# Experts' weights issued from two engines: ScalarE for the even units, SyncE for the odd units and each expert's first

## What is computed

```python
def moe_ffn(h, p, j):
    logits = (h @ p['w_router'][j] + p['b_router'][j]).astype(jnp.float32)
    top_v, top_i = lax.top_k(logits, TOP_K)                 # TOP_K = 2 of N_EXPERTS = 8
    gates = jax.nn.softmax(top_v, axis=-1)
    combine = jnp.einsum('blk,blke->ble', gates, one_hot(top_i))
    out = jnp.zeros_like(h)
    for e in range(N_EXPERTS):
        act = jax.nn.silu(h @ p['we_gate'][j, e]) * (h @ p['we_up'][j, e])   # 1024 x 1408 each
        out = out + combine[..., e:e + 1] * (act @ p['we_down'][j, e])       # 1408 x 1024
    return out
```

## Time and profile before

| | before |
|---|---|
| median of the runs (lowest, highest) | 924.25 us (922.62, 925.26) |
| profiled execution, its time | 925.9 us |
| profiled execution, its span | 924.2 us |
| mean granted TensorE clock | 0.977 |
| TensorE matmul busy | 874.5 us (95%) |
| VectorE busy | 711.6 us (77%) |
| ScalarE busy | 561.3 us (61%) |
| moved by DMA | 240.74 MB, mean 260 GB/s |
| first matmul of the experts to their last | 508.8 to 904.1 us |
| experts' units | 144: 104 of 1 MiB, 32 of 768 KB, 8 of 512 KB |

### The profile page before, as it was taken

The page is one execution under the profiler, slowest core; times in us unless marked ns, Lnnn a source line. Parts: engine busy times, 40 slices in busy tenths (PEclk is TensorE's granted clock), DMA queues, the critical chain, the costliest instruction groups (busy, mean ns, idle before and its releaser), DMA issues.

```text
span 924.2 us, 14135 instructions
## 1 busy us (share of the span) xinstructions
PE 874.5 (95%) x5414; PEld 778.2 (84%) x5414; DVE 711.6 (77%) x928; ACT 561.3 (61%) x633; POOL 47.0 (5%) x98
## 2 busy tenths in 40 slices
PE   4999999999999999999996999999999999999993
PEld 4997989999999999977885787888887888888881
DVE  4898895755546437978876889888888988888988
ACT  5427985444434335059952867686867777777751
POOL 2000012100000001010102000000000000000040
PEclk9999999999999999899997999999999999999998
DMA  8821137996345556510354789999999999999981
GB/s 332 338 92 44 42 129 290 395 418 249 135 176 212 185 177 251 224 48 1 112 221 162 271 316 391 376 357 385 371 382 341 390 368 389 371 385 355 378 312 49
DMA packets 39864, 240.74 MB, mean 260 GB/s; under 512 B 5016, under 2 KB 5368, under 8 KB 19056
## 3 DMA queue, kind: packets, MB, share of 16 engines
q1 hardware_dynamic: 32432, 208.01, 59.7%
q0 software_dynamic: 5936, 27.19, 7.6%
q10 hardware_dynamic: 1440, 4.77, 1.3%
HBM read 215.01 MB, written 25.51 MB: 260 GB/s over the span
## 4 chain that ended last, share of the span: by engine, by line
PE 80%; ACT 9%; DVE 7%; issue 2%; DMA 1%; DVEq 0%; ACTq 0%
PE ps L499 10%; PE ps L500 10%; PE ps L501 10%; PE ps L797 9%; PE ps L798 9%; PE ps L799 9%; PE ps L811 4%; PE ps L813 4%; PE ps L812 4%; PE ps L515 2%; ACT whi L926 1%; PE ps L872 1%; PE ps L449 1%; DVE low L336 1%; PE ps L819 1%
## 5 line engine op out<-in xcount | busy, mean ns | idle before, releaser
L1641 DVE TENSOR_TENSOR low<-raw,whi 128x2048 fp32r<-128x2048 f32 (+1 forms) x144 | 300.1, 2110 | 47.6 <-ACT whi L1160 47.2
L1160 ACT ACTIVATE whi<-raw 128x2048 fp32r<-128x2048 f32 (+1 forms) x144 | 252.9, 1781 | 74.7 <-DMA raw<-in_w_experts 54.9
L499 PE MATMUL ps<-nhi,whi 128*128 128x264 f32 x560 | 161.8, 289 | 16.8 <-DVE low L336 13.0
L926 ACT ACTIVATE whi<-raw 128x2048 fp32r<-128x2048 f32 (+1 forms) x60 | 109.2, 1826 | 109.9 <-PE ps L501 108.7
L336 DVE TENSOR_TENSOR low<-raw,whi 128x2048 fp32r<-128x2048 f32 (+1 forms) x60 | 130.5, 2180 | 45.5 <-ACT whi L926 45.4
L500 PE MATMUL ps<-nlo,whi 128*128 128x264 f32 x560 | 160.3, 286 | 0.0
L501 PE MATMUL ps<-nhi,low 128*128 128x264 f32 x560 | 159.6, 285 | 0.0
L797 PE MATMUL ps<-whi,ehi 128*128 128x512 f32 (+1 forms) x384 | 147.1, 383 | 0.2
L798 PE MATMUL ps<-low,ehi 128*128 128x512 f32 (+1 forms) x384 | 145.0, 378 | 0.0
L799 PE MATMUL ps<-whi,elo 128*128 128x512 f32 (+1 forms) x384 | 144.8, 377 | 0.0
L499 PEld LDWEIGHTS ps<-nhi,whi 128*128 128x128 f32 x560 | 106.5, 190 | 18.2 <-issue 16.8
(11 more groups left out here) (389 smaller groups left out, 1352.1 us busy)
## 6 DMA issues: line engine op xcount, KB each, us to landing
raw<-in_w_experts SPq DMA_DIRECT2D x104, 1024.0 KB, 6.9
raw<-in_w_dense SPq DMA_DIRECT2D x54, 1024.0 KB, 5.1
raw<-in_w_experts SPq DMA_DIRECT2D x32, 768.0 KB, 6.3
xs<-zero POOLq DMA_DIRECT2D x5, 2560.0 KB, 32.0
Cs<-in_state_c POOLq DMA_DIRECT2D x2, 2064.0 KB, 11.2
out_new_s<-Cs POOLq DMA_DIRECT2D x2, 2064.0 KB, 8.2
raw<-in_w_experts SPq DMA_DIRECT2D x8, 512.0 KB, 6.8
xe<-xs SPq DMA_DIRECT2D x7, 512.0 KB, 8.8
```

Of the source, the lines that this page charges most:

```text
L499: pe.matmul(o, hi[:, k, c], h_k, start=first, stop=False)
L926: act.activation(whi[:, u % NHI, 0:n], raw[:, u % NRAW, 0:n], ACT.Copy).then_inc(hi_done, 1)
L1160: act.activation(high_slot(odd, c)[:, 0:kt * w], raw[:, c % NRAW, 0:kt * w], ACT.Copy).then_inc(hi_done, 1)
L1641: dve.tensor_tensor(low[:, c % NRAW, part], raw[:, c % NRAW, part], high_slot(odd, c)[:, part].bitcast(F32), ALU.subtract).then_inc(lo_don ...
```

## The change

In the experts, the units with even numbers are issued by ScalarE. Each expert's unit 0 stays with SyncE, and so do units 0 to 5 of the first expert. ScalarE issues unit `c + 2` in `expert_hi` of unit `c`: first it waits for TensorE's unit `c - 4`, which is what frees both the high part's slot for unit `c` and the slot of `raw` for unit `c + 2`; then it issues the DMA; then it waits for unit `c`'s landing and converts it. For this the wait for `used` moves ahead of the wait for the landing, for all units. SyncE skips those units, and keeps the load of `xe` at its place.

```diff
+        def by_act(it, c):
+
+            return c % 2 == 0 and c > (NRAW - 1 if isinstance(it, int) and it == 0 else 0)
+
...
                         sp.dma_start(xe[:, :], block_of(xs, it + 1)).then_inc(S["xe_in"], 16)
+                    if by_act(it, c):
+                        continue
                     sp.wait_ge(used, it * NU + ND + c - NRAW + 1)
...
-            def expert_hi(it, c, odd=False):
+            def expert_hi(it, c, odd=False, e=None):
                 _, g, k0, kt, w = EU[c]
+                act.wait_ge(used, it * NU + ND + c - (3 if isinstance(it, int) and it == 0 and c < 3 else 4) + 1)
+                if e is not None and c + 2 < NU and by_act(it, c + 2):
+                    n = EU[c + 2][3] * EU[c + 2][4]
+                    src = a["w_experts"][bass.ds(e, 1), c + 2, :, 0:n].rearrange("o p n -> p (o n)")
+                    act.dma_start(raw[:, (c + 2) % NRAW, 0:n], src).then_inc(raw_in[(c + 2) % NRAW], 16)
                 act.wait_ge(raw_in[c % NRAW], it * (16 * NU // NRAW) + landed(ND - NRAW + c % NRAW) + 16 * (c // NRAW + 1))
-                act.wait_ge(used, it * NU + ND + c - (3 if isinstance(it, int) and it == 0 and c < 3 else 4) + 1)
                 act.activation(high_slot(odd, c)[:, 0:kt * w], raw[:, c % NRAW, 0:kt * w], ACT.Copy).then_inc(hi_done, 1)
...
-            def expert(it, odd=False, last=False):
+            def expert(it, e, odd=False, last=False):
...
-                        expert_hi(it, c, odd)
+                        expert_hi(it, c, odd, e)
```

## The result

The change makes the kernel slower: 948.75 us in the median of four runs (944.87 to 952.31), against 923.43 us before (four runs), a ratio of 1.0272 with a 95% interval of 1.024 to 1.0305. That is 25 us, where I had forecast 8.

The account below looks back on a forecast made before the run. TensorE was taken as the bound, with transfers right behind. Pauses of 8.5 us in five experts and 4.2 in the others, less 4.8 of old pauses, gave +7.9 us: 932 in the median, range 921 to 944.

Parts of the forecast that it names:

- Six units moved at no cost: ScalarE's queue: units 2, 4, 10, 12, 14 and 16 would cost 0, unit 2 lagging at most 0.4 us.
- the issue at no cost: On ScalarE, 62 issues would be covered by conversions or waits for landings: 0, against 31 us bare.
- the rival of two faster queues: Two read queues at about 420 GB/s instead of 373 would remove the 4.8 us of pauses: 919.5 us, chance 0.14.
- of each expert the largest lateness, not the sum: Per expert, lateness at one unit is slack for later ones, so only the largest counts: 1.7 or 1.4 us.
- Unit 14's pauses: TensorE's old pause of 0.96 us ahead of unit 14 would become 1.7 in five experts, 8.5 us.
- 1.3 us for unit 8: Issued behind the store, unit 8 would land at 628.5 in the third expert, 1.3 us late, contained in unit 6's 1.4.
- unit 6's 1.4: Issued behind the first SiLU, beside unit 7, unit 6 would land 1.4 us late if the rings share.
- Unit 8's limit: In the third expert, unit 8 had to land by 627.2, 4.6 us before its first matmul at 631.77.
- a third of the sharing: Unit 8's landing was put between arrival order (627.05) and an even share (631.3): 628.5.
- the old store's 8.2 us: The store's landing before the change, between even share (4.7) and arrival order (9.2), was read as nearer to arrival order.
- 12.7 us of pauses: TensorE's forecast pauses: 8.5 us in five experts with unit 14's pause, 4.2 at unit 6 in the others.
- The rings share evenly: Rival: unit 8 would be 4.1 us late in each of seven experts with a store, 949 us, chance 0.04.

Follow-up runs that it names:

- run 4: The changed kernel with units 6 and 8 given back to SyncE, ScalarE keeping its other six: 925.7 us, ratio 1.0023.
- run 13: The kernel before with ScalarE issuing unit 6 alone, behind the first SiLU, and SyncE's unit 7 waiting for that SiLU's end: 930.1 us, ratio 1.004.
- run 8: The kernel before, SyncE issuing all in one ring, unit 6 waiting for TensorE's unit 1 and the store directly ahead of unit 8: 930.5 us, ratio 1.0075.
- run 9: The kernel before with unit 6 alone issued by ScalarE, behind the first SiLU in the second ring: 939.8 us, ratio 1.0162.
- run 2: The changed kernel with unit 6 alone issued early, ahead of the first SiLU; unit 8 stays behind the store: 941.2 us, ratio 1.0152.
- run 10: The kernel before with unit 8 alone issued by ScalarE, directly behind the store: 927.2 us, ratio 1.0038.
- run 3: The kernel before, one ring, with SyncE's unit 6 waiting for TensorE's unit 1 in place of unit 0: 926.3 us, ratio 1.0029.
- run 7: The kernel before, one ring, with the store of the rows issued by SyncE directly ahead of unit 8: 923.6 us, ratio 0.9994.
- run 11: The kernel before with units 6 and 8 alone issued by ScalarE, both at their places in its order: 951.8 us, ratio 1.0308.
- run 14: The kernel before, one ring, with units 6 and 7 changing places in SyncE's order: 948.6 us, ratio 1.0287.
- run 16: The changed kernel with SyncE's unit 7 put behind unit 6 and unit 8 issued ahead of the store: 928.1 us, ratio 1.0045.
- run 5: The changed kernel with unit 8 alone issued ahead of the store; unit 6 stays behind the first SiLU: 936.1 us, ratio 1.0132.

## Why the prediction was wrong

**What held.** The direction, and the places: SiLU ahead of unit 6, the store ahead of unit 8, pauses ahead of both. Six units moved at no cost and the issue at no cost that run 4 can tell. No gain in rate: the windows show 333 to 368 GB/s for the second to seventh expert, before 362 to 380, so the rival of two faster queues is out, and the Trainium skill's rule (DMA: Bandwidth & Descriptors, Issuing engines are not separate DMA queues), that a second issuing engine saves only issue time, agrees with run 4, where the second ring brought nothing. Unit 6 was to land 7.85 us after issue if the rings shared, and it took 7.9 in the third expert; unit 8 was to take 9.6 and took 9.8 there, 10.5 in the median of the seven experts with a store.

**The step that failed first: of each expert the largest lateness, not the sum.** Unit 14's pauses were contained in the earlier ones: they are gone in seven experts, where I had 1.7 us in each of five. Unit 8's was not contained in unit 6's. Here the sum had 1.3 us for unit 8, under unit 6's 1.4. Unit 8's limit was too late by 0.6: I took the 4.6 us of a gate or up unit, but unit 8 also waits for flo, which stands behind its low part on VectorE. From the start of its conversion to TensorE the rows above show 634.44 to 639.63, 5.2 us. So it was late past unit 6's pause in six experts, 5.9 us together.

**The step under it: a third of the sharing.** It rested on the old store's 8.2 us between an even share (4.7) and the order of arrival (9.2). That was the wrong scale, because it had no place for packets that were issued earlier in the other ring and go first. Packets of the trace can be strung together, one engine's end to its next start, 16 strings at a time. Here is one of the 16 from each of four stretches, in the last the one that ended last (packets of 4 bytes are left out); `a` is 8 KB from SyncE's ring, `B` 8 KB from ScalarE's, `S` 4 KB of the store; a unit has eight packets on each engine:

```
before, third expert, from 617 us:    aaaaaaaaaaaaSaSaSaSaSaSaSaSaaaaaa
after, third expert, from 620.5 us:   aaaaaaaBaBaBaBBBBBSSSSSSSSBBBB
run 13, sixth expert, from 764 us:    BBBBBBBBaaaaaaaaaSaSaS
run 13, seventh expert, from 812.6:   aaaaaaaaBaBaBaBaBaBaBaBaSaSaS
```

In the kernel before, the store's first packet ran 3.5 us after its issue, behind packets of units 6 to 8, and from there it alternates with SyncE's ring, one packet each: eight of 0.16 and eight of 0.31 us are 3.8, and 3.5 + 3.8 = 7.3; its last packet ended 7.6 us after the issue. So the 8.2 us were a late start and then an even share, not something between. The Trainium skill's rule that I set aside (DMA: Bandwidth & Descriptors, Queues, rings and completion order) agrees with the alternating stretches, if its packet is one of these pieces, and not with the head start. In after's string the first two `a` are unit 5's; unit 7 has five of its eight packets through before unit 6 gets its first, then they alternate, then unit 6 ends, the store follows, and unit 8. In run 13's sixth expert unit 6 was first by 0.53 us and kept the engine for all eight. So in after unit 6 lands behind unit 7, or together with it, and TensorE needs it 2.8 us earlier. The rows by queue (packets, MB, share of the 16 engines' time) for the 8 us from unit 6's issue in after's third expert show the two rings side by side:

```profile
q10 hardware_dynamic: 212, 1.33, 49.1%
q1 hardware_dynamic: 167, 1.14, 40.0%
```

I had written that units 6 and 7 go within 0.2 us of each other, and counted unit 6 as late by 1.4; in the trace it is 1.8 in the mean of seven experts, 1.0 where unit 5 had landed 1.05 us after unit 6's issue, 3.56 where it took 2.1.

**What the sum did not have.** A pause was priced at its own length. The three units at 1.2 GHz add 4.4 us and the restarts 2.8.

**The sum again.** Forecast: 12.7 us of pauses, less 4.8. Found: 12.6 ahead of unit 6, 7.5 elsewhere (unit 8's 5.9 foremost), less 4.8, and 7.2 of longer matmuls: 22.5, for the 22.7 between the windows. So what the forecast lacked is about half the pauses elsewhere and half the longer matmuls. That 12.7 and 12.6 agree is luck: 8.5 of the 12.7 stood at unit 14, and unit 6 is late by 1.8 and not 1.4, in seven experts and not in eight. The forecast of +7.9 is near the time of the same order in one ring (run 8, 7 us), in the number alone: there the pauses are ahead of unit 8.

**The rival that had the number.** "The rings share evenly" gave 949, at 0.04. Its time is right and its account is not: it has 28.7 us at unit 8 and 1.4 at unit 6, and the trace has 5.9 and 12.6. Its rule, though, was the right one behind the late start, and the store's row, read packet by packet, would have said so before the change.

**Where first come did not help.** Both units land together in some experts, 10 us and more after issue, whichever went first. In run 13's seventh expert the packets show how: 121 of unit 6's 128 have ended 4.5 us after its issue, and the last seven end from 5.5 to 9.7, every second packet of one engine (the fourth string). On that engine unit 5 ended only 2.0 us after unit 6's issue, and from there the two rings alternate. Unit 6's landing, at 10.3, goes by that last engine.

**What stays open.** Why one engine is so late with unit 5. In after and in runs 9 and 13 unit 5 landed 2.1 us or more after unit 6's issue in each expert in which both units took 10 us, but the fourth expert of run 13 with 2.2 took only 7.3, and no run changed this alone. And why run 2 costs 14 us while run 10 costs 4: in run 2 the issue of unit 8 itself slips to 2 to 3 us behind its slot's release in the fourth to the seventh expert, with unit 4 landing late (8.3 to 9.4 us after issue there, 4.7 to 7.1 in the kernel before); that ScalarE's lag feeds on itself there is argued from the trace, not shown by a run.

## What to carry to other kernels

Transfers that are needed in a fixed order should be issued in that order, most simply in one ring. The same lateness cost less there than with a second ring: 3 us and 15 for unit 6 (runs 3 and 9), nothing and 4 for unit 8 (runs 7 and 10), 7 and 28 for both (runs 8 and 11), because in two rings a late transfer lands behind or beside one that is needed after it. It is the order that counts: one ring in the wrong order cost 26 (run 14), two rings with the order put right 4 (run 16). If a second issuing engine must be used, look at what stands ahead of each issue in its order, and at which of two issues a few tenths of a microsecond apart comes first. A pause of a tensor engine that has no slack costs more than its length: here 15.3 us of new pauses brought 7.2 us of longer matmuls with them.

## What the hardware showed that I had not expected

- Two rings alternate packet by packet, but an issue 0.53 us ahead can keep the engines for its whole eight packets (4.7 us to landing, the shortest of the earlier trace rows), and an issue 0.17 us behind waits for five of the other's eight in after's third expert. One engine of 16 that is still at work on the unit before undoes the head start (10.3 us).
- In after, TensorE's clock fell to 1.2 GHz behind pauses of 2.03, 2.31 and 3.56 us and in no expert behind its pauses of up to 1.88 us. A unit then took about 1.5 us longer. The length of the pause alone does not decide: the clock fell behind one of 1.86 us in run 9's sixth expert, and did not behind one of 2.83 in run 5's eighth.
- Two units changed in one ring's order (run 14) cost 26 us of 924, with not a byte more to move.
